# Smaller score tiles, sums in four column tiles, and a reordered weight part in a three-block layer stack

## The chip, the cores and the metric

One core of one Trainium2 chip. The metric is the device time of one execution in microseconds; the number given for a kernel is the median of its runs.

## What is computed

Three layers on 256 tokens of width 1024, in f32: an even block (HGRN2 scan and retention, then a squared-ReLU MLP), an odd block (mLSTM, then an MLP), and a hybrid layer (gated delta rule and block attention). The change touches the HGRN2 scan of the even block, some sums over partitions, and the preparation of a triangular inverse in the delta rule:

```python
def hgrn2_scan(q, k, logf, v):            # even block, 4 heads of 128, chunks of 64
    ...
        bcum = jnp.cumsum(lfc, axis=2)
        diff = bcum[:, :, :, None, :] - bcum[:, :, None, :, :]
        decay = jnp.exp(jnp.where(mask[:, :, None], diff, -jnp.inf))
        scores = jnp.einsum('bhtd,bhsd,bhtsd->bhts', qc, kc, decay)
...
    f = lb + (1.0 - lb) * jax.nn.sigmoid(hf)      # q = silu(hq), k = 1 - f, logf = log(f)
...
    # gated delta rule (hybrid layer), chunks of 64
    a = jnp.where(strict, jnp.einsum('bhnid,bhnjd->bhnij', k_beta, kf) * decay, 0.0)
    t_inv = lax.linalg.triangular_solve(eye + a, eye, left_side=True, lower=True)
```

## The kernel before, in words

**Projections.** The program is one fixed order per engine, written out by hand. All weights are cut into tiles of 128 partitions by 2048 columns (1 MB), loaded by SP into five slots `raw`. Every tile is split in two: ScalarE writes the high part `w_hi` (`split_until` of the scalar block, L1408, four slots), VectorE subtracts it from the tile and writes the low part `w_lo` (`split_until` of the vector block, L1915, 2.3 us each). TensorE multiplies by the high part first (`high_tile`) and, after a wait for the low part (`low_tile`), by that. Feature-major projections (`project_feature_major`, L583, L584 and the low part L591) serve hf, hq, rq, rk and, in the last block, dk, dq, dv, bq, bk; token-major ones (`project_token_major`, L625, L626, low part L632) serve the rest. Each projection has two weight tiles, named here bk.0 and bk.1. Where in VectorE's order the low part of a tile stands is said by a call `split_until(n)`, which makes all low parts up to tile n.

**Scores of the even block.** The 64x64 decayed score blocks can't be one product, since the decay depends on the feature. They are summed over levels m = 1, 2, 4, ... 128: for a pair of neighbouring runs of m tokens, the query side is scaled by exp(b - b at the edge) and the key side by exp(b at the edge - b). For each level VectorE writes the exponents into `D` (`diffs`, L2152 and L2153, one instruction for each half of the pairs), ScalarE takes exp (`level_exp`, L1617), VectorE multiplies by q and k into `Z0` or `Z1` (`scaled`, L2179 and L2180), TensorE makes the scores (`level_scores`, L965 for levels 0 to 6, blocks of 64x64: 16 matmuls of 128 rows by 64 columns, in two column tiles), and VectorE takes from them what the level's mask selects (`keep`, L2201, a predicated copy of 512 columns). Level 0 is q and k undecayed. The levels stand between the halves of the projections hi to rv0, from 38 to 100 us. Before them come the forget gate f (four instructions L2132, from it k by L2136), its logarithm (ScalarE, L1609), the scans of b (L2141) and the scaling of q (L2208).

**Sums over partitions** are matmuls with a column of ones as the moving side: four conditioning sums (`ada_sum`, L884, 8 matmuls each, between the products of the first and second MLP), the denominators of the odd block (L1108, 24 matmuls) and two sums of squares (`sum_squares` of the tensor block, L1140, 16 each). All use 64 stationary columns.

**The inverse in the delta rule.** VectorE multiplies keys' products by decays (`at`, L2567), copies the 32x32 diagonal blocks into the compact tile `ac` (L2569, four copies of 32 partitions), announces `at_ready`, makes the first inverse `Y32` (L2573, L2575) and its transpose `X` (L2576). GpSimd masks the compact tile for four levels (L546, `am_ready`). Before this it adds three shifted copies for a convolution (L537) and clears two areas with memsets (L541, L542, `zero_ready`). TensorE meanwhile projects bq and bk, transposes v (`dvt`, L1156) and then, between the halves of bv and bz, makes the small products with `X`, masks and `Y32` (L1227, L1233: 32x32 matmuls in four tiles; L1241, L1249, L1254 on the larger levels). In VectorE's order the low part of bk.0 (`split_until(LAST["dv"] + 3)`) stands behind the transpose.

Of the kernel before, what the change touches and what calls it, by code (L numbers as in the profile page):

```python
# [30 lines left out]
H = 4  # L31
# [192 lines left out]
E_AT = dict(qs=0, k=1024, b=2048, D=3072, Z0=4096, Z1=5120, scd=6144, sco=7168, vhg=7680, rq=8704, rk=9728,  # L224
# [19 lines left out]
def build(nc, weights, cols, rows, const, const_even, masks, x_in, out, stop=None):  # L244
    with ExitStack() as ctx:
# [190 lines left out]
        f_gate_ready = sem("f_gate_ready")  # L436
# [89 lines left out]
        def _(pool):  # L526
# [3 lines left out]
            for i in range({"even": 1, "mlp0": 2, "odd": 3, "mlp1": 4}.get(stop, 6)):  # L530
                if i == 5:
# [22 lines left out]
        def _(pe):  # L554
# [321 lines left out]
            def ada_sum(name):  # L876
# [63 lines left out]
            def level_scores(l):  # L940
# [162 lines left out]
            for t in range(TT):  # L1103
                for h in range(H):
                    for s in range(t + 1):
                        for b in range(2):
                            o = pair("mden")[64 * b:64 * b + 64, t * H + h:t * H + h + 1]
                            mm = pe.matmul(o, pt(h, s, t)[:, 64 * b:64 * b + 64], ones[:, 0:1], start=(s == 0), stop=(s == t))  # L1108
# [26 lines left out]
            def sum_squares(src):  # L1135

                after(l2_sq)
                for i in range(8):
                    for b in range(2):
                        mm = pe.matmul(acc[64 * b:64 * b + 64, i:i + 1], at(src, 64, i * P + 64 * b), ones[:, 0:1],  # L1140
# [60 lines left out]
            head_transposes("dvt", "v")  # L1201
            after(at_ready)
            fill("bk", 1)
# [185 lines left out]
        def _(act):  # L1389
# [218 lines left out]
            after(f_gate_ready)  # L1608
            act.activation(ev("D"), ev("Z0"), ACT.Ln).then_inc(logf_ready, 1)  # L1609
# [5 lines left out]
            def level_exp():  # L1615
                after(diff_ready)
                act.activation(ev("D"), ev("D"), ACT.Exp).then_inc(decay_ready, 1)  # L1617
# [29 lines left out]
            level_exp()  # L1647
            split_until(9)
            scaled_out("hi", by_token(ev("vhg")))
            level_exp()  # L1650
            split_until(10)
            level_exp()
            split_until(11)
            level_exp()
            scaled_out("hg", by_token(ev("ghg")), ACT.Silu)
            split_until(12)
            level_exp()
            split_until(13)
            level_exp()
            split_until(14)  # L1660
            swap_halves("rq")
            level_exp()
            split_until(15)
            level_exp()
# [215 lines left out]
        def _(dve):  # L1880
# [230 lines left out]
            def forget_bound():  # L2111
# [5 lines left out]
                link(dve.tensor_scalar(stat[:, 60:64], stat[:, 84:88], -1.0, 1.0, ALU.mult, ALU.add))  # L2117
# [12 lines left out]
            after(z0_ready)  # L2130
            for h in range(H):
                ins = dve.tensor_scalar(ev("Z0", T, h * T), ev("Z0", T, h * T), stat[:, 60 + h:61 + h], stat[:, 84 + h:85 + h],  # L2132
                                        ALU.mult, ALU.add)
            ins.then_inc(f_gate_ready, 1)
            dve.wait_ge(f_gate_ready, 1)
# [608 lines left out]
```

## Time and profile before

| | |
|---|---|
| median of 3 runs | 891.84 us (891.81 to 892.28) |
| profiled execution | 891.87 us, of it 890.1 us from the first to the last instruction |
| mean granted TensorE clock | 0.996 |
| PE / DVE / ACT / POOL busy | 878.5 / 644.6 / 497.4 / 21.6 us |
| DMA | 165.48 MB, mean 186 GB/s |

PE is TensorE, DVE VectorE, ACT ScalarE, POOL GpSimd; L12 is line 12 of the kernel. Rows of a timeline begin with start and length in microseconds; an f32 matmul shows as two passes, so 16 matmuls are x32.

### The profile page before, as it was taken

To read this page: it belongs to the slowest core of one execution; us is meant where nothing else is said; L and a number is where in the kernel's file an instruction comes from. 1 tells how busy PE (TensorE), PEld (TensorE's weight loads), DVE (VectorE), ACT (ScalarE), POOL (GpSimd) and SP (SyncE) were. 2 spreads that over 40 slices of the span, in tenths; PEclk is the share of its full clock that TensorE was granted. 3 is DMA by queue.
4 is the path that set the end of the run, shared out by engine and by line. 5 is a ranking of instruction groups with operands and counts; after the bars stand their busy time and mean duration, and the time that the engine had idled before them with its cause. 6 is when DMAs were issued, how large, how long until landed. Compare 5 with 4: busy or idle time off the path is not lost.

```text
span 890.1 us, 13545 instructions
## 1 busy us (share of the span) xinstructions
PE 878.5 (99%) x5714; PEld 749.5 (84%) x5714; DVE 644.6 (72%) x793; ACT 497.4 (56%) x678; POOL 21.6 (2%) x21
## 2 busy tenths in 40 slices
PE   9999999999999999999999999999999989999997
PEld 7889888888888888898888888888879988788885
DVE  6999656569777776699576977776677894556655
ACT  6875557466444444666566644445468764466624
POOL 0000000000000000000000000000000070000000
PEclk9999999999999999999999999999999999999999
DMA  9745444466666665454346666666446424434331
GB/s 363 275 143 176 156 142 141 143 236 221 239 232 236 235 238 184 173 182 148 137 142 230 227 236 235 236 239 237 147 154 236 143 95 149 144 120 158 135 128 48
DMA packets 24172, 165.48 MB, mean 186 GB/s; under 512 B 2688, under 2 KB 2944, under 8 KB 4912
## 3 DMA queue, kind: packets, MB, share of 16 engines
q1 hardware_dynamic: 22608, 159.74, 50.2%
q0 software_dynamic: 1072, 4.39, 1.3%
q8 instruction: 45, 0.74, 0.3%
q10 hardware_dynamic: 432, 0.49, 0.2%
q14 instruction: 15, 0.12, 0.0%
HBM read 163.56 MB, written 1.05 MB: 185 GB/s over the span
## 4 chain that ended last, share of the span: by engine, by line
PE 88%; DVE 8%; ACT 2%; issue 1%; DVEq 0%; ACTq 0%
PE acc L643 30%; PE lin L604 11%; PE lin L625 6%; PE lin L609 6%; PE lin L632 6%; PE lin L626 6%; DVE w_lo L1915 3%; PE lin L591 3%; PE lin L583 3%; PE lin L584 3%; PE acc L851 1%; PE acc L735 1%; PE acc L736 1%; DVE arena L2368 1%; ACT w_hi L1408 1%; PE acc L745 1%
## 5 line engine op out<-in xcount | busy, mean ns | idle before, releaser
L1915 DVE TENSOR_TENSOR w_lo<-raw,w_hi 128x2048 fp32r<-128x2048 f32 x137 | 315.0, 2313 | 141.6 <-ACT w_hi L1408 140.9
L1408 ACT CAST w_hi<-raw 128x2048 fp32r<-128x2048 f32 x137 | 259.5, 1907 | 137.1 <-DMA raw<-in_weights 89.8
L643 PE MATMUL acc<-w_hi,f_hi 128*128 128x512 f32 x288 | 113.2, 393 | 0.0
L643 PE MATMUL acc<-w_hi,f_lo 128*128 128x512 f32 x288 | 112.4, 390 | 0.0
L625 PE MATMUL lin<-w_hi,h_both 128*128 128x512 f32 x272 | 110.0, 404 | 0.6 <-ACT arena L1630 0.5
L604 PE MATMUL lin<-h_both,w_hi 128*128 128x512 f32 x448 | 106.7, 390 | 0.0
L626 PE MATMUL lin<-w_hi,h_both 128*128 128x512 f32 x272 | 106.3, 391 | 0.0
L604 PEld LDWEIGHTS lin<-h_both,w_hi 128*128 128x128 f32 x448 | 83.2, 188 | 16.8
L643 PE MATMUL acc<-w_lo,f_hi 128*128 128x512 f32 x288 | 79.0, 389 | 0.0
L632 PE MATMUL lin<-w_lo,h_both 128*128 128x512 f32 x272 | 69.2, 390 | 0.2 <-DVE w_lo L1915 0.2
L583 PE MATMUL lin<-h_both,w_hi 128*128 128x256 f32 x272 | 67.3, 287 | 0.0
L584 PE MATMUL lin<-h_both,w_hi 128*128 128x256 f32 x272 | 66.1, 283 | 0.0
L643 PEld LDWEIGHTS acc<-w_lo,f_hi 128*128 128x128 f32 x288 | 54.1, 188 | 11.3
L643 PEld LDWEIGHTS acc<-w_hi,f_hi 128*128 128x128 f32 x288 | 54.1, 188 | 10.8 <-DVE f_lo L2326 0.2
L643 PEld LDWEIGHTS acc<-w_hi,f_lo 128*128 128x128 f32 x288 | 54.1, 188 | 10.7
L625 PEld LDWEIGHTS lin<-w_hi,h_both 128*128 128x128 f32 x272 | 51.1, 188 | 12.3 <-issue 0.7
L632 PEld LDWEIGHTS lin<-w_lo,h_both 128*128 128x128 f32 x272 | 50.9, 188 | 11.5 <-DVE w_lo L1915 0.9
L626 PEld LDWEIGHTS lin<-w_hi,h_both 128*128 128x128 f32 x272 | 51.1, 188 | 9.7
L609 PEld LDWEIGHTS lin<-h_both,w_lo 128*128 128x128 f32 x448 | 57.4, 191 | 2.2
L643 PE MATMUL acc<-w_hi,h_both 128*128 128x512 f32 x224 | 58.2, 393 | 0.0
L609 PE MATMUL lin<-h_both,w_lo 128*128 128x256 f32 x448 | 58.1, 283 | 0.0
L583 PEld LDWEIGHTS lin<-h_both,w_hi 128*128 128x128 f32 x272 | 52.1, 191 | 0.3
(382 smaller groups left out, 1197.0 us busy)
## 6 DMA issues: line engine op xcount, KB each, us to landing
raw<-in_weights SPq DMA_DIRECT2D x149, 1024.0 KB, 4.8
rowbuf<-in_rows POOLq DMA_DIRECT2D x6, 512.0 KB, 4.0
x<-in_x_in SPq DMA_DIRECT2D x2, 512.0 KB, 4.4
raw<-in_weights SPq DMA_DIRECT2D x2, 512.0 KB, 6.7
arena<-in_const_even POOLq DMA_DIRECT2D x1, 1024.0 KB, 11.8
out<-x SPq DMA_DIRECT2D x3, 256.0 KB, 2.1
cst<-in_const SPq DMA_DIRECT2D x1, 596.0 KB, 10.0
out<-x ACTq DMA_DIRECT2D x1, 256.0 KB, 2.1
```

Of the source, the lines that this page charges most:

```text
L583: pe.matmul(o, hi[:, w], h[0], start=b == 0 and k == 0, stop=False)
L584: pe.matmul(o, hi[:, w], h[1], start=False, stop=False)
L591: mm = pe.matmul(pair(name)[:, (2 * i + b) * T:(2 * i + b + 1) * T], lo[:, w], chunk(k)[0], start=False, stop=b == 1 and k == DC - 1)
L604: pe.matmul(pair(out)[:, b * 512:(b + 1) * 512], hi[:, k * 256 + b * P:k * 256 + (b + 1) * P], h_both[:, k, :, :].rearrange("p a t -> p (a ...
L609: mm = pe.matmul(pair(out)[:, b * 512:b * 512 + T], lo[:, k * 256 + b * P:k * 256 + (b + 1) * P], h_hi[:, k, :], start=False, stop=k == DC ...
L625: pe.matmul(o, h[0], hi[:, w], start=i == 0 and k == 0, stop=False)
L626: pe.matmul(o, h[1], hi[:, w], start=False, stop=False)
L632: mm = pe.matmul(pair(name)[:, t * 512:(t + 1) * 512], chunk(4 * i + k)[0][:, t * P:(t + 1) * P], lo[:, k * 512:(k + 1) * 512], start=Fals ...
L643: return pe.matmul(acc[:, at:at + 512], part_of(2 * j + k)[i][:, t * P:(t + 1) * P], w[:, k * 1024 + c * 512:k * 1024 + (c + 1) * 512], st ...
L735: pe.matmul(lead_sum(t), h_hi[:, k, t * P:(t + 1) * P], w, start=k == 0, stop=False)
L1408: act.copy(w_hi[:, o % SPLIT, :], raw[:, j % RAW, :]).then_inc(hi_done, 1)
L1915: dve.tensor_tensor(w_lo[:, j % RAW, :], r, hi.bitcast(F32), ALU.subtract).then_inc(tile_split, 1)
```

## The change

1. `level_scores`: levels 0 to 5 in blocks of 32x32, 32 matmuls of 128 rows by 32 columns in four column tiles; level 6 by its 32x32 off-diagonal blocks alone, 16 matmuls in two column tiles; levels 7 and 8 as before. `keep` works on 256 columns; the level 6 blocks are copied straight to their place, and the near blocks are put there at level 7 by four small copies.
2. `ada_sum`, the denominators and `sum_squares`: four column tiles of 32 instead of two of 64, so twice the matmuls.
3. `diffs` is one instruction over both halves; the signs go into the scale of two exponentials; `scaled` is one product over both halves, which reads q and k through one access pattern (their places are swapped for it). At levels 7 and 8 copies of b go: the exponential reads b itself.
4. f is no longer written: ScalarE takes Ln(scale * sigmoid + bias) per head, VectorE makes k from the sigmoid in four instructions.
5. Last block: bk.0's low part ahead of the compact copies on VectorE; GpSimd's memsets behind its mask products; TensorE's wait for the compact tile behind bk.1.

```diff
@@ pool
-                    pool.memset(arena[:, S_AT["Y"]:S_AT["Y"] + 1024], 0.0)
-                    pool.memset(arena[0:64, S_AT["X64"]:S_AT["X64"] + 512], 0.0).then_inc(zero_ready, 1)
                     pool.wait_ge(at_ready, 1)
                     for l in range(2, 6):
...
+                    pool.memset(arena[:, S_AT["Y"]:S_AT["Y"] + 1024], 0.0)
+                    pool.memset(arena[0:64, S_AT["X64"]:S_AT["X64"] + 512], 0.0).then_inc(zero_ready, 1)
@@ ada_sum (the denominators and sum_squares in the same way)
-                    for b in range(2):
-                        at = c * P + 64 * b
-                        mm = pe.matmul(pair(name)[64 * b:64 * b + 64, c:c + 1], a[:, at:at + 64], ones[:, 0:1], start=True, stop=True)
+                    for r in range(4):
+                        at = c * P + 32 * r
+                        mm = pe.matmul(pair(name)[32 * r:32 * r + 32, c:c + 1], a[:, at:at + 32], ones[:, 0:1], start=True, stop=True)
@@ level_scores
+                elif l == 6:
+                    for i in range(8):
+                        for b in range(2):
+                            o = acc[64 * b:64 * b + 32, a + 32 * i:a + 32 * (i + 1)]
+                            c = i * P + 64 * b
+                            mm = pe.matmul(o, k[:, c:c + 32], q[:, c + 32:c + 64], start=True, stop=True)
                 else:
                     for i in range(8):
-                        for b in range(2):
-                            o = acc[64 * b:64 * b + 64, a + 64 * i:a + 64 * (i + 1)]
-                            c = i * P + 64 * b
-                            mm = pe.matmul(o, k[:, c:c + 64], q[:, c:c + 64], start=True, stop=True)
+                        for r in range(4):
+                            o = acc[32 * r:32 * r + 32, a + 32 * i:a + 32 * (i + 1)]
+                            c = i * P + 32 * r
+                            mm = pe.matmul(o, k[:, c:c + 32], q[:, c:c + 32], start=True, stop=True)
@@ tensor, last block
             head_transposes("dvt", "v")
+            fill("bk", 1)
             after(at_ready)
-            fill("bk", 1)
@@ scalar
-            act.activation(ev("D"), ev("Z0"), ACT.Ln).then_inc(logf_ready, 1)
+            for h in range(H):
+                ins = act.activation(ev("D", T, h * T), ev("Z0", T, h * T), ACT.Ln, scale=stat[:, 60 + h:61 + h],
+                                     bias=stat[:, 84 + h:85 + h])
...
+                if m < 64:
+                    d = ev("D").rearrange("p (n a m) -> p n a m", a=2, m=m)
+                    act.activation(d[:, :, 1, :], d[:, :, 1, :], ACT.Exp)
+                    act.activation(d[:, :, 0, :], d[:, :, 0, :], ACT.Exp, scale=-1.0).then_inc(decay_ready, 1)
+                    return
@@ vector, diffs and scaled
-                    edge = b[:, :, 0, m - 1:m].to_broadcast([P, n, m])
-                    dve.tensor_tensor(d[:, :, 1, :], b[:, :, 1, :], edge, ALU.subtract)
-                    dve.tensor_tensor(d[:, :, 0, :], edge, b[:, :, 0, :], ALU.subtract).then_inc(diff_ready, 1)
+                    edge = b[:, :, m - 1:m].to_broadcast([P, n, 2 * m])
+                    dve.tensor_tensor(d, b, edge, ALU.subtract).then_inc(diff_ready, 1)
...
-                dve.tensor_tensor(z[:, :, 1, :], d[:, :, 1, :], q[:, :, 1, :], ALU.mult)
-                dve.tensor_tensor(z[:, :, 0, :], d[:, :, 0, :], k[:, :, 0, :], ALU.mult).then_inc(z_ready, 1)
+                kq = ev("k", 2 * (1024 + m)).rearrange("p (a r) -> p a r", a=2)[:, :, 0:1024]
+                kq = kq.rearrange("p a (n x m) -> p n a x m", x=2, m=m)[:, :, :, 0, :]
+                dve.tensor_tensor(z, d, kq, ALU.mult).then_inc(z_ready, 1)
@@ vector, keep
-                dve.copy_predicated(ev("sco", 512).rearrange("p (n t) -> p n t", n=8), msk_l, src).then_inc(level_free, 1)
+                msk_l = small_mask(l).to_broadcast([P, 8, 32])
+                dve.copy_predicated(near.rearrange("p (n t) -> p n t", n=8), msk_l, src).then_inc(level_free, 1)
@@ vector, last block
             link(dve.tensor_tensor(at("at"), at("at"), acc[:, 0:1024], ALU.mult))
+            split_until(LAST["dv"] + 3)
             for r in range(4):
                 ins = dve.tensor_copy(compact(at("ac", 256), r), small_blocks(at("at"), r))
...
-            split_until(LAST["dv"] + 3)
             split_until(LAST["bq"] + 3)
```

What moves, on the engines it concerns. VectorE in the last block, from the second product of the scores to q's scaling, before (`w_lo<-raw,w_hi` is a weight tile's low part, here bk.0, bk.1, bv.0):

```order
L2566 TENSOR_TENSOR arena<-arena,acc 128x1024 [waits sc_done]
L2567 TENSOR_TENSOR arena<-arena,acc 128x1024
L2569 COPY arena<-arena 32x256 [waits dve_step]
L2569 COPY arena<-arena 32x256 x3
L2573 TENSOR_TENSOR arena<-arena,msk 128x256 [waits at_ready]
L2575 TENSOR_TENSOR arena<-cst,arena 128x256 [waits dve_step]
L2576 STREAM_TRANSPOSE arena<-arena 128x256 [waits dve_step]
L1915 TENSOR_TENSOR w_lo<-raw,w_hi 128x2048 [waits hi_done] x3
L2583 TENSOR_TENSOR arena<-arena 128x512 [waits deg_read,l2_done]
```

and the same piece in the changed kernel:

```order
L2594 TENSOR_TENSOR arena<-arena,acc 128x1024 [waits sc_done]
L2595 TENSOR_TENSOR arena<-arena,acc 128x1024
L1941 TENSOR_TENSOR w_lo<-raw,w_hi 128x2048 [waits hi_done,dve_step]
L2598 COPY arena<-arena 32x256 x4
L2602 TENSOR_TENSOR arena<-arena,msk 128x256 [waits at_ready]
L2604 TENSOR_TENSOR arena<-cst,arena 128x256 [waits dve_step]
L2605 STREAM_TRANSPOSE arena<-arena 128x256 [waits dve_step]
L1941 TENSOR_TENSOR w_lo<-raw,w_hi 128x2048 [waits hi_done] x2
L2611 TENSOR_TENSOR arena<-arena 128x512 [waits deg_read,l2_done]
```

One low part of three has moved ahead of the four copies, and everything from the copies to the transpose stands behind it. GpSimd in the same place, before:

```order
L537 TENSOR_TENSOR arena<-arena 128x4x253 [waits taps_ready,v_conv]
L541 MEMSET arena 128x1024 [waits even_loaded,v_conv]
L542 MEMSET arena 64x512
L546 TENSOR_TENSOR arena<-arena,msk 128x256 [waits at_ready]
L546 TENSOR_TENSOR arena<-arena,msk 128x256 x3
```

and changed:

```order
L537 TENSOR_TENSOR arena<-arena 128x4x253 [waits taps_ready,v_conv]
L544 TENSOR_TENSOR arena<-arena,msk 128x256 [waits at_ready,even_loaded,v_conv]
L544 TENSOR_TENSOR arena<-arena,msk 128x256 x3
L545 MEMSET arena 128x1024
L546 MEMSET arena 64x512
```

The memsets now follow the four mask products. VectorE in the even block, from the scans of b to the exponents of level 2, before:

```order
L2141 SCALAR_TENSOR_TENSOR arena<-cst,arena 128x256 x4
L2152 TENSOR_TENSOR arena<-arena 128x512
L2153 TENSOR_TENSOR arena<-arena 128x512
L2208 TENSOR_TENSOR arena<-lin,arena 128x1024
L1915 TENSOR_TENSOR w_lo<-raw,w_hi 128x2048 x3
L2179 TENSOR_TENSOR arena<-arena 128x512
L2180 TENSOR_TENSOR arena<-arena 128x512
L2152 TENSOR_TENSOR arena<-arena 128x256x2
L2153 TENSOR_TENSOR arena<-arena 128x256x2
L2201 COPY_PREDICATED arena<-msk,acc 128x512
```

and changed:

```order
L2166 SCALAR_TENSOR_TENSOR arena<-cst,arena 128x256 x4
L2176 TENSOR_TENSOR arena<-arena 128x1024
L2236 TENSOR_TENSOR arena<-lin,arena 128x1024
L1941 TENSOR_TENSOR w_lo<-raw,w_hi 128x2048 x3
L2202 TENSOR_TENSOR arena<-arena 128x1024
L2176 TENSOR_TENSOR arena<-arena 128x1024
L2229 COPY_PREDICATED arena<-msk,acc 128x256
```

The order is the same; pairs of instructions have become one, and the predicated copy is half as wide.

## Rows read from the trace of the kernel before

**Rows 1.** The page, part 1: busy us (share of the span) xinstructions.
```profile
PE 878.5 (99%) x5714; PEld 749.5 (84%) x5714; DVE 644.6 (72%) x793; ACT 497.4 (56%) x678; POOL 21.6 (2%) x21
```

**Rows 2.** Waits of TensorE: us in total, times, longest us; first and fifth of eight.
```profile
PE lin L591 <- DVE w_lo L1915: 2.4, 1, 2.4
...
PE acc L1254 <- DVE arena L2599: 0.3, 1, 0.3
```

**Rows 3.** Timeline of TensorE, even block: start us, us, instruction, xcount.
```profile
36.37 2.14 PE L632 MATMUL lin<-w_lo,h_both 128*128 128x512 f32 x8
38.44 1.15 PE L965 MATMUL acc<-arena 128*64 128x64 f32 x32
...
51.94 1.15 PE L965 MATMUL acc<-arena 128*64 128x64 f32 x32
```

**Rows 4.** Timeline of TensorE, last block: 32x32 matmuls in four tiles, two, one.
```profile
747.99 0.75 PE L1227 MATMUL acc<-arena 32*32 32x32 f32 x64
...
769.75 0.69 PE L1241 MATMUL acc<-arena 32*32 32x32 f32 x32
...
773.85 0.57 PE L1249 MATMUL acc<-arena 32*32 32x32 f32 x13
```

**Rows 5.** Timeline of TensorE: sums over partitions.
```profile
253.65 0.63 PE L884 MATMUL lin<-cst,ada_acc 128*64 128x1 f32 x16
...
432.02 1.57 PE L1108 MATMUL lin<-cst,arena 128*64 128x1 f32 x48
...
682.56 1.10 PE L1140 MATMUL acc<-cst,arena 128*64 128x1 f32 x32
```

**Rows 6.** Timeline of VectorE, last block: low parts and the compact copies.
```profile
715.29 4.54 DVE L1915 TENSOR_TENSOR w_lo<-raw,w_hi 128x2048 fp32r<-128x2048 f32 x1
...
722.13 3.73 DVE L2569 COPY arena<-arena 32x256 f32<-32x256 f32 x4
...
727.54 2.28 DVE L1915 TENSOR_TENSOR w_lo<-raw,w_hi 128x2048 fp32r<-128x2048 f32 x1
```

**Rows 7.** The chain that ended last: low parts of bk.0 and bk.1.
```profile
729.88 3.59 PE lin L591 x16
738.29 1.93 PE lin L591 x16
```

**Rows 8.** Stretches: us, busy us (x) of PE, PEld, DVE, ACT, POOL, PEclk, DMA share, GB/s.
```profile
725.00:730.00 5.00, 2.61 (x22) 2.41 (x22) 4.88 (x7) 4.14 (x6) 4.47 (x4) 1.00 0.53 195
730.00:735.00 5.00, 5.00 (x30) 5.00 (x31) 5.00 (x2) 0.52 (x3) 3.03 (x2) 0.66 0.17 28
```

**Rows 9.** GpSimd: its additions by line (ns min/median/max, first and last start), then its timeline.
```profile
L537 POOL TENSOR_TENSOR arena<-arena x3: 1982/2397/3937, 715.3 to 721.8; 128x1020 f32<-128x1020 f32 x1, 128x1016 f32<-128x1016 f32 x1, 128x1012 f32<-128x1012 f32 x1
...
723.82 0.98 POOL L541 MEMSET arena<- 128x1024 f32 x1
724.74 0.67 POOL L542 MEMSET arena<- 64x512 f32 x1
725.94 7.09 POOL L546 TENSOR_TENSOR arena<-arena,msk 128x256 f32<-128x256 f32 x4 [0.53 <-DVE arena L2569]
```

**Rows 10.** Timeline of VectorE, even block.
```profile
34.03 6.69 DVE L1915 TENSOR_TENSOR w_lo<-raw,w_hi 128x2048 fp32r<-128x2048 f32 x3
...
48.15 0.69 DVE L2180 TENSOR_TENSOR arena<-arena 128x512 f32<-128x512 f32 x1
...
50.09 0.74 DVE L2201 COPY_PREDICATED arena<-msk,acc 128x512 f32<-128x512 uint16 x1
...
58.58 1.22 DVE L2232 TENSOR_TENSOR arena<-arena 128x1024 f32<-128x1024 f32 x1
```

**Rows 11.** Timeline of ScalarE: the logarithm, and four activations with a column scale.
```profile
27.60 1.06 ACT L1609 ACTIVATE arena<-arena 128x1024 f32<-128x1024 f32 x1
...
718.50 1.71 ACT L1797 ACTIVATE arena<-arena,colbuf 128x256 f32<-128x256 f32 x4
```

**Rows 12.** One stretch of the even block, columns as in rows 8.
```profile
30.00:60.00 30.00, 30.00 (x250) 24.51 (x250) 28.03 (x29) 22.91 (x20) 0.00 (x0) 1.00 0.49 169
```

More of the change, by code:

```diff
@@ L434, in build @@
         s_out = sem("s_out")
-        f_gate_ready = sem("f_gate_ready")
+        bound_ready = sem("bound_ready")
         logf_ready = sem("logf_ready")
@@ L1105, in _ @@
                     for s in range(t + 1):
-                        for b in range(2):
-                            o = pair("mden")[64 * b:64 * b + 64, t * H + h:t * H + h + 1]
-                            mm = pe.matmul(o, pt(h, s, t)[:, 64 * b:64 * b + 64], ones[:, 0:1], start=(s == 0), stop=(s == t))
+                        for r in range(4):
+                            o = pair("mden")[32 * r:32 * r + 32, t * H + h:t * H + h + 1]
+                            mm = pe.matmul(o, pt(h, s, t)[:, 32 * r:32 * r + 32], ones[:, 0:1], start=(s == 0), stop=(s == t))
             mm.then_inc(lin_special, 1)
@@ L1138, in sum_squares @@
                 for i in range(8):
-                    for b in range(2):
-                        mm = pe.matmul(acc[64 * b:64 * b + 64, i:i + 1], at(src, 64, i * P + 64 * b), ones[:, 0:1],
+                    for r in range(4):
+                        mm = pe.matmul(acc[32 * r:32 * r + 32, i:i + 1], at(src, 32, i * P + 32 * r), ones[:, 0:1],
                                        start=True, stop=True)
@@ L1613, in _, with level_exp @@
             ahead("hq")
-            def level_exp():
+            def level_exp(l):
                 after(diff_ready)
-                act.activation(ev("D"), ev("D"), ACT.Exp).then_inc(decay_ready, 1)
+                m = (LEVELS + [128])[l - 1]
+                if m < 64:
[3 more added lines that the diff above has]
+                    return
+                b, d = (ev(x).rearrange("p (h c m) -> p h c m", c=4, m=64) for x in ("b", "D"))
+                if m == 64:
+                    for c in (0, 2):
+                        act.activation(d[:, :, c + 1, :], b[:, :, c + 1, :], ACT.Exp)
+                    d = ev("D").rearrange("p (n a m) -> p n a m", a=2, m=m)
+                    act.activation(d[:, :, 0, :], d[:, :, 0, :], ACT.Exp).then_inc(decay_ready, 1)
+                else:
+                    act.activation(d[:, :, 2, :], b[:, :, 2, :], ACT.Exp)
+                    act.activation(d[:, :, 0:2, :], d[:, :, 0:2, :], ACT.Exp)
+                    act.activation(d[:, :, 3, :], d[:, :, 3, :], ACT.Exp).then_inc(decay_ready, 1)
             def swap_halves(name):
@@ L2161, in diffs @@
                     for c in (0, 2):
-                        dve.tensor_tensor(d[:, :, c, :], end(c), b[:, :, c, :], ALU.subtract)
-                        ins = dve.tensor_copy(d[:, :, c + 1, :], b[:, :, c + 1, :])
+                        ins = dve.tensor_tensor(d[:, :, c, :], end(c), b[:, :, c, :], ALU.subtract)
                 else:
@@ L2177, in scaled @@
                     dve.wait_ge(level_done, l - 1)
[L2178 to L2180 removed]
+                z, d = (ev(x).rearrange("p (n a m) -> p n a m", a=2, m=m) for x in (f"Z{l % 2}", "D"))
+                kq = ev("k", 2 * (1024 + m)).rearrange("p (a r) -> p a r", a=2)[:, :, 0:1024]
+                kq = kq.rearrange("p a (n x m) -> p n a x m", x=2, m=m)[:, :, :, 0, :]
+                dve.tensor_tensor(z, d, kq, ALU.mult).then_inc(z_ready, 1)
                 dve.wait_ge(z_ready, l + 1)
[L2183 to L2184 removed]
+            near = ev("sco", 256)
             def keep(l):
@@ L2193, in keep @@
                 if l == 7:
-                    for b in range(2):
-                        link(dve.tensor_copy(own_blocks(ev("scd"), b), low_levels(b)))
+                    for r in range(4):
+                        ins = dve.tensor_copy(small_blocks(ev("scd"), r), compact(near, r))
+                    link(ins)
                     upper = acc[0:64, a:a + 512].rearrange("p (n t) -> p n t", n=8)
@@ L2198, in keep @@
                     return
-                src = acc[:, a:a + 512].rearrange("p (n t) -> p n t", n=8)
-                msk_l = level_mask(l).rearrange("p (o t) -> p o t", o=1).to_broadcast([P, 8, 64])
-                dve.copy_predicated(ev("sco", 512).rearrange("p (n t) -> p n t", n=8), msk_l, src).then_inc(level_free, 1)
+                src = acc[:, a:a + 256].rearrange("p (n t) -> p n t", n=8)
+                if l == 6:
+                    for b in range(2):
+                        dst = ev("scd")[64 * b:64 * b + 32, :].rearrange("p (n t) -> p n t", n=8)[:, :, 64 * b + 32:64 * b + 64]
+                        ins = dve.tensor_copy(dst, src[64 * b:64 * b + 32, :, :])
+                    ins.then_inc(level_free, 1)
+                    return
+                msk_l = small_mask(l).to_broadcast([P, 8, 32])
+                dve.copy_predicated(near.rearrange("p (n t) -> p n t", n=8), msk_l, src).then_inc(level_free, 1)
                 dve.wait_ge(level_free, l + 1)
```

40 lines of the change are left out of this document (18 added, 22 removed).

## The prediction, made before the changed kernel ran

> **What bounds the kernel now.** I read the page's shares first: TensorE has matmuls in flight in 99% of the span, VectorE works 72% of it, ScalarE 56% [rows 1]. Then the waits of TensorE: the list has eight lines, 5.6 us together, and its first, 2.4 us for a low weight part, is nearly half of that [rows 2]. So what TensorE issues sets the time. A microsecond off TensorE's own work is a microsecond off the end, wherever VectorE and ScalarE can follow; a microsecond off the other two is worth nothing, except in front of that one wait. The sum is made against the profiled execution, 891.87 us (890.1 of span and 1.8 around it); the median of the runs shown, 891.84, is the same for this purpose. A difference under 0.2% (1.8 us) can't be told from none here.
>
> **Small matmuls.** Every f32 matmul appears as two passes. A 64-wide score level is 16 matmuls, 32 passes, and its row spans 1.15 us with a last pass of 0.22: a pass starts every (1.15 - 0.22)/31 = 0.030 us [rows 3]. These are two column tiles that run side by side on the same 128 rows. How fast 32-wide tiles go is seen in the last block, where tiles of 32 rows by 32 columns are used: four tiles in turn make (0.75 - 0.19)/63 = 0.0089 us per pass, two make (0.69 - 0.19)/31 = 0.0161, one makes (0.57 - 0.19)/12 = 0.032 [rows 4]. So one tile takes 0.032 us for its pass and the tiles overlap. The new shape, 128 rows by 32 columns, stands in no row. Its upper neighbour is the pair of 64-wide tiles (0.030 per pass), its lower one the four 32x32 tiles (0.0089). I take 0.0089 for four column tiles, because the 64-wide pair already shows that column tiles on shared rows overlap; both ends stay for the range.
> - Levels 0 to 5: 16 matmuls become 32, 64 passes; the row becomes 63 x 0.0089 + 0.19 = 0.75 us. 6 x (1.15 - 0.75) = **2.40 us** saved.
> - Level 6: 16 matmuls stay, now 32 wide in two column tiles. By the two-tile row 0.69 us: **0.46 us** saved. Levels 7 and 8 are unchanged.
> - Sums over partitions have one moving column, and the rows show that this doesn't help: they too start a pass every 0.029 us [rows 5], so the 64-wide stationary side sets the pace, not the moving one. In four tiles: four conditioning sums, 15 x 0.029 = 0.44 becomes 31 x 0.0089 = 0.28, **0.64** in all; the denominators, 47 x 0.029 = 1.37 becomes 95 x 0.0089 = 0.85, **0.52**; two sums of squares, 31 x 0.029 = 0.90 becomes 0.56, **0.68**.
> Together 4.70 us of TensorE.
>
> The Trainium skill speaks against this part: "TensorEngine Tiling (Array Packing)", Performance Considerations, warns not to take a tiling factor from a dimension that is small already, since every matmul carries some 60 cycles, and "TensorE: Matmul & The Clock Gate", Part 1, says that starts never come closer than about 25 ns. The trace of this kernel disagrees for 32x32 tiles (8.9 ns between starts). By that rule the six levels and the sums, 736 passes, would take an estimated 18.4 us of starts and the forecast would end near 895.
>
> **The low part ahead of the compact copies.** VectorE works in order. Between the products L2567 and the low part of bk.0 stand four copies into the compact tile (3.73 us), two small operations and a transpose; the low part starts at 727.54 and ends at 729.82 [rows 6]. TensorE had finished the high half of bk.0 at 727.5 and waits 2.4 us for it, until 729.88 [rows 2, 7]. The clock follows: the granted clock is 1.00 in 725 to 730 and 0.66 in 730 to 735, a mean over the two levels of 2.4 and 1.2 GHz [rows 8], and the 16 matmuls behind the wait take 3.59 us, where the 16 of bk.1 take 1.93 [rows 7]: 1.66 too much.
>
> After the change this subtraction is at the head, at 722.13. GpSimd's third shifted addition starts at 721.8 and takes 1.98 us [rows 9], and beside such additions VectorE's subtraction of bq.1 took 4.54 us for what otherwise takes 2.28 [rows 6]; the first copy suffers from the same now. So I let the moved subtraction wait until 723.8 and end at 726.05. TensorE comes for it at 727.5, less what it gains by then over VectorE, at most the 0.34 us of the second sum of squares. The margin is about 1 us: the wait goes, **2.4 + 1.66 = 4.06 us**. Late next are the copies. The two memsets of GpSimd (0.98 and 0.67 us) that ran beside them are now behind its four mask products, so the copies take at most the old 3.73: the compact tile is ready between 726.1 and 729.8 instead of 725.9, X 1.7 us later (725.86 to 727.54 now), the first mask about a quarter of 7.09 later [rows 6, 9]. TensorE comes for bk.1's low part at 727.5 + 1.93 + 4.82 = 734.2 (the last term is what lies between the low parts of bk.0 and bk.1 now, 738.29 - 729.88 - 3.59 [rows 7]), and for the first small products two us behind that. The low part of bk.1, behind the transpose, ends between 730 and 734: enough, but this is the margin to look at. The cleared areas are wanted only from 769 on, and GpSimd is through at about 738. TensorE's wait for the compact tile moves behind bk.1 and costs nothing for the same reason.
>
> **The even block's VectorE and ScalarE work.** Differences of both halves in one: 0.69 + 0.69 (1.30 by the starts) becomes about 1.22, the row of one 1024-wide product; the products z the same; the predicated copy of 512 columns, 0.74, halves to some 0.4; copies at levels 7 and 8 go, the four small ones at level 7 replace two of 0.42. That is some 3 us less for VectorE between 30 and 100 us, where it is nearly full (28.03 us of 30 in the first stretch) [rows 12]. All of it is costed at nothing for the end: VectorE had z for level 2 ready at 48.8 and TensorE wanted it at 51.9 [rows 3, 10]; if that cover were gone, each 0.1 us would count once per level. ScalarE's logarithm in four pieces with a column as scale and bias costs 1.71 instead of 1.06, by the row of four 256-wide activations with a column scale [rows 11], so 0.22 for each added instruction; its exponential in two or three pieces is then 0.2 to 0.4 us longer per level, hidden by the same 3 us. The logarithm has no such cover: scans, differences and q behind it end about 0.1 us later, and TensorE takes the low part of hi.0 at 36.37, when VectorE has just finished it (34.03 plus a third of 6.69 = 36.26) [rows 3, 10]. I give 0.1 us for this and 0.1 for the other short waits [rows 2] that become longer when TensorE comes earlier.
>
> Sum: 4.70 + 4.06 - 0.2 = 8.56 us. 891.87 - 8.56 = **883.3 us**.
>
> **The rivals.**
> A. *Four column tiles on shared rows don't run four wide.* Each tile needs all 128 partitions read for itself. If what limits the 64-wide pair is columns delivered per microsecond (64 in 0.029), a 32-wide pass costs 0.0145, levels 0 to 5 and all sums gain nothing, and only level 6 and the wait do: 891.87 - 4.06 - 0.46 + 0.2 = 887.6. For it: passes with 1 and with 64 moving columns cost the same. Against: the clean overlap of the 32x32 tiles [rows 4], though these lie on different rows.
> B. *A wait comes back.* The moved subtraction, held up by GpSimd, or bk.1's low part comes late enough to idle TensorE and lower its clock again: the 4.06 us are lost, 891.87 - 4.70 + 0.2 = 887.4. Against: the margins of 1 and of 0 to 4 us above. With A as well it is 891.6, no change.
> C. *A floor between starts for tiles of 128 rows, whatever their width.* The 0.029 with one moving column could be that floor. Then twice the passes cost twice the time: levels 0 to 5, 6 x (63 x 0.029 + 0.19 - 1.15) = 5.2; conditioning sums 4 x 0.46 = 1.9; denominators 1.4; sums of squares 2 x 0.93 = 1.9: 10.4 us more, 4.06 less, 898.2, slower than before. It decides from a pass of about 0.020 us on: there 736 passes and their tails eat the 4.06 and level 6's 0.46. Against: one 32x32 tile alone needs 0.032 and four need 0.0089 each, which no floor allows, unless it belongs to tiles of 128 rows.
> The Trainium skill's 25 ns is a milder form of C and shares its chance.
>
> **How the numbers follow.** Forecast 0.70, since two independent pieces of it rest on rows; A 0.12; B 0.10; A and B together 0.03; C 0.05. Faster by over 0.2%: forecast, A and B, 0.92. Same: 0.03. Slower: 0.05. The range reaches from 882.3 (a pass every 0.032/4 = 0.008 us, 0.7 less, and no new short waits) to 887.9, which takes in A and B.
>
> **What would show it.** Score rows of levels 0 to 5 at x64 with 0.75 us each, level 6 at 0.69, denominators x96 near 1.0; at 1.1 us a level it is A, at 2.0 it is C. No wait of TensorE for the low part of bk.0, granted clock 1.00 throughout from 10 to 880 us, and L591 of bk.0 at 1.9 us. On VectorE, bk.0's subtraction ends before TensorE's high half does, and the copies follow it. Wrong would be: a new line in TensorE's waits over 0.5 us, in the even block (ScalarE's pieces) or at bk.1, or a saved 4.7 us that turns up as idle time ahead of a low part.

## The result, and the profile after

The changed kernel takes 883.54 us (median of 5 runs, 883.44 to 884.02), the kernel before 891.84: a ratio of 0.9912 with a 95% interval of 0.9900 to 0.9923. In a later round, beside the experiments, it took 883.43 (883.31 to 883.56). The profiled execution took 883.74 us, 881.9 of it span. Beside the experiments the kernel before took 891.5 to 893.1 us in 28 executions, with a mean granted clock of at most 0.997, and 890.2 to 890.4 us in 11, with 0.998 or 0.999 (one more, at 1082.8 us and 0.752, is left out), so the 8.3 us are a difference from the more frequent group.

The page, part 1, of the changed kernel (answers to [rows 1]):

```profile
PE 871.8 (99%) x6082; PEld 742.3 (84%) x6082; DVE 640.2 (73%) x779; ACT 499.6 (57%) x691; POOL 21.3 (2%) x21
```

TensorE is busy for 6.7 us less, with 368 passes more. Its waits, five of nine lines (to [rows 2]): the 2.4 us for bk.0's low part are gone, and L632 has grown from 0.2 to 0.4. The two lines of L895 are waits for the first loads; another trace of the same kernel, that of experiment 6, has neither.

```profile
PE lin L625 <- ACT arena L1656: 0.5, 1, 0.5
PE lin L632 <- DVE w_lo L1941: 0.4, 2, 0.2
PE acc L895 <- DMA x<-in_x_in: 0.4, 1, 0.4
PE acc L1260 <- DVE arena L2627: 0.3, 1, 0.3
...
PE acc L895 <- DMA cst<-in_const: 0.2, 1, 0.2
```

Its timeline: hi.0's low part, a score level (L971), level 6 (L965), a conditioning sum, the denominators, a sum of squares (to [rows 3, 5]).

```profile
36.85 1.45 PE L632 MATMUL lin<-w_lo,h_both 128*128 128x512 f32 x5 [0.24 <-DVE w_lo L1941]
38.92 0.76 PE L971 MATMUL acc<-arena 128*32 128x32 f32 x64
...
83.72 0.70 PE L965 MATMUL acc<-arena 128*32 128x32 f32 x32
...
251.40 0.43 PE L884 MATMUL lin<-cst,ada_acc 128*32 128x1 f32 x32
...
429.19 0.98 PE L1114 MATMUL lin<-cst,arena 128*32 128x1 f32 x96
...
678.88 0.71 PE L1146 MATMUL acc<-cst,arena 128*32 128x1 f32 x64
```

The level's row is (0.76 - 0.20)/63 = 0.0089 us per pass, the denominators' (0.98 - 0.17)/95 = 0.0085, a last pass of 0.20 or 0.17 taken off. Four column tiles on the same 128 rows start passes as closely as the four 32x32 tiles did before. The first line is new: 0.24 us of wait for hi.0's low part.

The chain that ended last and the stretches, around bk.0 (to [rows 7, 8]): its 16 low matmuls take 1.92 us, and the clock stays at its upper level.

```profile
723.39 1.92 PE lin L591 x16
...
730.02 1.93 PE lin L591 x16
```

```profile
715.00:725.00 10.00, 10.00 (x85) 10.00 (x85) 9.82 (x12) 8.04 (x11) 6.50 (x5) 1.00 0.56 207
725.00:730.00 5.00, 5.00 (x45) 5.00 (x44) 5.00 (x3) 3.85 (x10) 5.00 (x3) 1.00 0.65 211
```

VectorE's timeline there, then GpSimd's (to [rows 6, 9]):

```profile
717.78 3.75 DVE L1941 TENSOR_TENSOR w_lo<-raw,w_hi 128x2048 fp32r<-128x2048 f32 x1
721.46 1.18 DVE L2598 COPY arena<-arena 32x256 f32<-32x256 f32 x4
...
723.95 0.45 DVE L2605 STREAM_TRANSPOSE arena<-arena 128x256 f32<-128x256 f32 x1
724.32 4.96 DVE L1941 TENSOR_TENSOR w_lo<-raw,w_hi 128x2048 fp32r<-128x2048 f32 x2
```

```profile
722.81 7.00 POOL L544 TENSOR_TENSOR arena<-arena,msk 128x256 f32<-128x256 f32 x4 [3.42 <-DVE arena L2598]
729.76 0.96 POOL L545 MEMSET arena<- 128x1024 f32 x1
730.65 0.52 POOL L546 MEMSET arena<- 64x512 f32 x1
```

The moved subtraction takes 3.75 us, stretched by GpSimd's addition, and ends at 721.5; TensorE comes for it at 723.2. The four copies, with nothing of GpSimd beside them, take 1.18 us instead of 3.73.

The even block, where the new 0.24 us come from: ScalarE's logarithm, then VectorE's scans, differences and q (to [rows 11, 10]).

```profile
27.65 2.08 ACT L1617 ACTIVATE arena<-arena,stat 128x256 f32<-128x256 f32 x4
```

```profile
29.77 2.44 DVE L2166 TENSOR_TENSOR_SCAN arena<-cst,arena 128x256 f32<-128x256 f32 x4 [1.03 <-ACT arena L1617]
32.24 1.23 DVE L2176 TENSOR_TENSOR arena<-arena 128x1024 f32<-128x1024 f32 x1
33.38 1.22 DVE L2236 TENSOR_TENSOR arena<-lin,arena 128x1024 f32<-128x1024 f32 x1
34.51 6.69 DVE L1941 TENSOR_TENSOR w_lo<-raw,w_hi 128x2048 fp32r<-128x2048 f32 x3
```

Four logarithms with columns as scale and bias take 2.08 us, not the 1.71 of activations with a scale column alone. VectorE now waits for them, and q is scaled half a microsecond later than before (33.38 us for 32.89), the low part behind it as well.

### The profile page after: what moved, and what is told of

It is laid out like the page before. It is cut to its first block, busy times and chain, and to the rows that moved or that the text cites. A ratio compares the mean times of both kernels' runs of the same rounds, so it can differ in the third digit from the quotient of the medians.

```text
span 881.9 us, 14281 instructions
## 1 busy us (share of the span) xinstructions
PE 871.8 (99%) x6082; PEld 742.3 (84%) x6082; DVE 640.2 (73%) x779; ACT 499.6 (57%) x691; POOL 21.3 (2%) x21
## 3 DMA queue, kind: packets, MB, share of 16 engines
HBM read 163.56 MB, written 1.05 MB: 187 GB/s over the span
## 4 chain that ended last, share of the span: by engine, by line
PE 88%; DVE 7%; ACT 3%; issue 1%; DMA 1%; DVEq 0%; SPq 0%; ACTq 0%
PE acc L643 30%; PE lin L604 12%; PE lin L625 6%; PE lin L609 6%; PE lin L632 6%; PE lin L626 6%; PE lin L583 3%; DVE w_lo L1941 3%; PE lin L584 3%; PE lin L591 3%; PE acc L851 1%; PE acc L735 1%; PE acc L736 1%; DVE arena L2396 1%; ACT w_hi L1414 1%
## 5 line engine op out<-in xcount | busy, mean ns | idle before, releaser
L632 PE MATMUL lin<-w_lo,h_both 128*128 128x512 f32 x272 | 69.2, 390 | 0.4 <-DVE w_lo L1941 0.4
L632 PEld LDWEIGHTS lin<-w_lo,h_both 128*128 128x128 f32 x272 | 50.9, 188 | 11.9 <-DVE w_lo L1941 1.3
```

Source lines behind the costliest of these rows:

```text
L632: mm = pe.matmul(pair(name)[:, t * 512:(t + 1) * 512], chunk(4 * i + k)[0][:, t * P:(t + 1) * P], lo[:, k * 512:(k + 1) * 512], start=Fals ...
```

## Experiments

Theory: the gain is TensorE's own shorter rows plus the vanished wait with its slow clock, and all else is covered. Rivals: one of the two is worth nothing and the other more, or VectorE's relief did it. Medians of 4 to 5 runs (11 for the exchanged loops); the changed kernel, 883.43 and 883.54 in two rounds, is the mark, and the runs of one version spread by 0.1 to 0.7 us. The experiments ran on four chips, and the mark beside them on one of these alone (experiment 6 and the first trials of 7); the medians of the kernel before on the four, 891.78 to 891.93, agree within 0.15 us, so versions on different chips are compared to a few tenths at best. Ratios are to the kernel before. Every kernel does the whole computation.

**1. The low part back** in its old place, in the changed kernel.

```diff
-            split_until(LAST["dv"] + 3)
             for r in range(4):
                 ins = dve.tensor_copy(compact(at("ac", 256), r), small_blocks(at("at"), r))
...
             dve.transpose(at("X", 256), at("Y32", 256)).then_inc(X_ready, 1)
+            split_until(LAST["dv"] + 3)
             split_until(LAST["bq"] + 3)
```

> The changed kernel with bk.0's low part back behind the transpose, all else as changed. Theory: in the changed kernel TensorE comes for this low part at 723.2 us. With the copies first again, held up by GpSimd's addition until 719.4, but with no memset beside them, the low part would end at about 724.6, so TensorE waits about 1.4 us: 883.5 + 1.4 = 884.9 us if the granted clock stays at 1.00, up to 1.7 more (886.6) if it falls behind the wait as it did before. Rival (the order on VectorE was worth nothing, the gain was in the matmuls): 883.5.

Measured 885.09 us (884.86 to 885.35), ratio to before 0.993 (0.9918 to 0.9942): 1.6 more than the changed kernel, near the 1.4 of the theory without a fall of the clock. Timelines of VectorE and TensorE, and the stretch:

```profile
718.20 2.67 DVE L2597 COPY arena<-arena 32x256 f32<-32x256 f32 x4
```

```profile
724.88 2.18 PE L591 MATMUL lin<-h_both,w_lo 128*128 128x256 f32 x16 [1.05 <-DVE w_lo L1941]
```

```profile
725.00:730.00 5.00, 5.00 (x43) 5.00 (x44) 5.00 (x2) 2.52 (x10) 4.39 (x4) 1.00 0.34 113
```

The copies are 1.1 us shorter than before without the memsets beside them (2.67 for 3.73), so the wait is 1.05 us instead of 2.4, and after 1.05 us of idle the granted clock did not fall. The row behind the wait is 2.18 us long, where the same row in the changed kernel takes 1.92: this wait cost some 0.25 us more than its idle time, at the upper clock. So the rows give 1.3 us for the move and the runs 1.6. This profiled execution was also 0.4 us late before it came to the place (its first matmul of hi.0 starts at 33.22 us, that of the changed kernel at 32.80); in the trace of experiment 6, the changed kernel again, it is 32.55, so this start isn't the same in every execution. That moving the memsets alone would have brought the rest is read off these rows; it was not run.

**2. The low part moved alone**, in the kernel before (the same edit the other way).

> The kernel before with this one move alone: bk.0's low part ahead of the compact copies on VectorE, memsets and matmuls untouched. Theory: the wait of 2.4 us and the half clock behind it (1.7 us) go: 891.8 - 4.1 = 887.7 us, and the granted clock is 1.00 from 10 to 880 us. Rival 1 (the wait only moves on to bk.1's low part or to the compact tile): 889 to 892 with a new wait of TensorE there. Rival 2 (the clock fall has another cause than the wait): 889.4, with a stretch of half clock that stays.

Measured 887.65 us (887.53 to 888.14), ratio 0.9959 (0.9947 to 0.9972): 4.1 less than before, to a tenth what was expected. TensorE's waits have no L591 any more, and the stretch that had 0.66 has 1.00:

```profile
730.00:735.00 5.00, 5.00 (x45) 5.00 (x43) 5.00 (x4) 3.97 (x9) 4.13 (x2) 1.00 0.62 211
```

No wait took its place in the last block, and the half clock went with the wait. The two can now be priced apart. Between the start of bk.0's low row and the end of the transposes of v behind it lie 4.57 us in the kernel before (3.59 and 0.98) and 3.05 in experiment 1 (2.18 and 0.87), which had a wait but no half clock: the clock costs 1.5 us, the wait 2.4 and 0.25. The 11 executions of the kernel before with the higher mean clock are 1.6 us shorter (medians of 890.3 and 891.9), about what the fall costs; it was probably missing there. No trace of one was kept, so this is not shown.

**3. The sums in two column tiles again**, in the changed kernel; one of three places:

```diff
-                    for r in range(4):
-                        at = c * P + 32 * r
-                        mm = pe.matmul(pair(name)[32 * r:32 * r + 32, c:c + 1], a[:, at:at + 32], ones[:, 0:1], start=True, stop=True)
+                    for b in range(2):
+                        at = c * P + 64 * b
+                        mm = pe.matmul(pair(name)[64 * b:64 * b + 64, c:c + 1], a[:, at:at + 64], ones[:, 0:1], start=True, stop=True)
```

> The changed kernel with all sums over partitions in two column tiles of 64 again. By the starts of the passes in the two traces (29.1 ns before, 8.5 now): conditioning sums 4 x 0.20, denominators 0.59, sums of squares 2 x 0.39 = 2.2 us more: 885.7 us. Rival (sums that stand ahead of a wait give nothing back): the two sums of squares and the denominators cost nothing, only the conditioning sums do: 884.3.

Measured 885.36 us (885.26 to 885.85), ratio 0.9935 (0.9921 to 0.9948): 1.8 to 1.9 more, where starts alone gave 2.2 and the rival 0.8. Counted to the start of the next matmul, the rows of its trace are 2.16 us longer (0.56 for 0.36 four times, 1.49 for 0.91, 1.03 for 0.64 twice). The sums give back most of their time; where the other 0.3 us went is not shown.

**4. Score levels in 64x64 blocks again**, in the changed kernel, with the predicated copies that belong to them (`level_scores` for levels 0 to 6 and `keep` as before).

> The changed kernel with the scores of levels 0 to 6 in 64x64 blocks and the predicated copies of 512 columns as before; sums, logarithm, merged instructions and the moved low part as changed. Theory: per level 0 to 5 the last pass starts 0.93 us behind the first instead of 0.57, and the next matmul 0.152 behind it instead of 0.126, so 0.39 each; level 6 0.93 instead of 0.50, 0.45: 2.8 us more, 883.5 + 2.8 = 886.3. Rival (VectorE, loaded with 0.3 us more per predicated copy, now makes TensorE wait): over 887, with waits in the even block.

Measured 886.38 us (886.34 to 886.66), ratio 0.9945 (0.9932 to 0.9958): 2.8 to 2.9 more, as expected. The wait for hi.0 is there too (0.24 us), and no other has come in the even block, so it doesn't hang on the tiles.

**5. Column tile after column tile.** The same 32 matmuls a level, the loops exchanged.

```diff
-                    for i in range(8):
-                        for r in range(4):
+                    for r in range(4):
+                        for i in range(8):
```

> The changed kernel with the loops of levels 0 to 5 exchanged: all eight 32x32 blocks of one column tile, then the next, so neighbours in the order use the same tile. Same 32 matmuls. Theory: the tiles overlap only when neighbouring instructions go to different tiles; a pass every 0.032 us as in the row of one 32x32 tile, 63 x 0.032 + 0.2 = 2.2 us a level instead of 0.77: 6 x 1.4 = 8.6 us more: 892.1. Rival (TensorE picks matmuls of other tiles ahead out of its queue): a level stays near 0.77, total 883.5.

Measured 890.36 us (890.18 to 890.92), ratio 0.999 (0.9982 to 0.9999): 6.8 to 6.9 more, most of what the change had won and far above the 2.8 that the smaller blocks gave: in this order they are slower than the old 64x64 blocks (1.91 us a level for 1.15). TensorE's timeline, a level:

```profile
39.08 1.91 PE L971 MATMUL acc<-arena 128*32 128x32 f32 x64
```

That is (1.91 - 0.20)/63 = 0.027 us per pass instead of 0.0089, and six levels times 1.15 us make the 6.9. The overlap comes from neighbours in the order going to different tiles, and the engine did not look ahead for them. The expectation had 0.032 from a 32-row tile; a tile of 128 rows is faster, 0.027. Four tiles in turn are thus three times as quick as one, not four times; what holds them at 0.0089 is not shown.

**6. The mark again, and halves apart.** The even block's differences, exponentials and products as before the change.

```diff
-                    b, d = (ev(x).rearrange("p (n c) -> p n c", n=n) for x in ("b", "D"))
-                    edge = b[:, :, m - 1:m].to_broadcast([P, n, 2 * m])
-                    dve.tensor_tensor(d, b, edge, ALU.subtract).then_inc(diff_ready, 1)
+                    b = ev("b").rearrange("p (n a m) -> p n a m", a=2, m=m)
+                    d = ev("D").rearrange("p (n a m) -> p n a m", a=2, m=m)
+                    edge = b[:, :, 0, m - 1:m].to_broadcast([P, n, m])
+                    dve.tensor_tensor(d[:, :, 1, :], b[:, :, 1, :], edge, ALU.subtract)
+                    dve.tensor_tensor(d[:, :, 0, :], edge, b[:, :, 0, :], ALU.subtract).then_inc(diff_ready, 1)
...
```

> The changed kernel itself, as the mark for the runs beside it on the same chip: 883.5 us.

Measured 883.43 us (883.31 to 883.56), ratio 0.9907 (0.9893 to 0.9920).

> The changed kernel with the even block's differences, exponentials and products as before (two differences and two products of half the size a level, one exponential over all, the copies at levels 7 and 8 back); score tiles, predicated copies and logarithm as changed. Theory: the merged instructions were worth nothing for the end, since z is ready about 3 us before TensorE wants it: 883.5, within 0.3. Rival (VectorE is nearly full between 30 and 90 us, so its 3 us less are what let TensorE come earlier): up to 1 to 2 us slower, with waits of TensorE for VectorE in the even block.

Measured 883.61 us (883.43 to 883.88), ratio 0.9909 (0.9895 to 0.9922): 0.2 more than the mark beside it, and the two sets of runs overlap. Point 3 of the change is worth nothing that is clear of the spread. Its instructions did get cheaper: VectorE's timeline with the halves apart, then that of the changed kernel, for the same level.

```profile
60.58 0.69 DVE L2161 TENSOR_TENSOR arena<-arena 128x512 f32<-128x512 f32 x1
61.19 0.68 DVE L2162 TENSOR_TENSOR arena<-arena 128x512 f32<-128x512 f32 x1
```

```profile
60.50 1.23 DVE L2176 TENSOR_TENSOR arena<-arena 128x1024 f32<-128x1024 f32 x1
61.64 0.44 DVE L2229 COPY_PREDICATED arena<-msk,acc 128x256 f32<-128x256 uint16 x1
```

The narrower predicated copies stay here, and the merged instructions stay in experiment 4; no run takes both away. It is shown that VectorE can do without either of them, and not that it can do without both.

**7. Can the new 0.24 us go?** First trial: q's scaling ahead of level 1's differences.

```diff
-            diffs(1)
             filled(dve, "hq")
             dve.tensor_tensor(by_head(ev("qs")), by_head(pair("hq")[:, :]), every, ALU.mult).then_inc(freed("hq"), 1)
+            diffs(1)
```

> The changed kernel with the differences of level 1 behind the scaling of q. In the changed kernel TensorE waits 0.24 us for hi.0's low part, because the logarithm in four pieces (2.08 us) delays scans, differences and q. Theory: q's scaling starts at 32.9 instead of 33.4, and the wait shrinks to at most 0.1 us: 883.3. Rival: the scans still end too late, or the exponentials of level 1 come late instead: 883.5.

Measured 884.35 us (884.32 to 884.38), ratio 0.9917 (0.9903 to 0.9930): 0.9 slower than the mark, against the expectation. VectorE's timeline and TensorE's:

```profile
32.85 1.22 DVE L2235 TENSOR_TENSOR arena<-lin,arena 128x1024 f32<-128x1024 f32 x1 [0.90 <-PE lin L591]
33.99 1.22 DVE L2176 TENSOR_TENSOR arena<-arena 128x1024 f32<-128x1024 f32 x1
35.12 6.69 DVE L1941 TENSOR_TENSOR w_lo<-raw,w_hi 128x2048 fp32r<-128x2048 f32 x3
```

```profile
37.46 2.14 PE L632 MATMUL lin<-w_lo,h_both 128*128 128x512 f32 x8 [1.10 <-DVE w_lo L1941]
```

VectorE now idles 0.90 us for TensorE's hq and does the differences between q and the low part that TensorE wants. The expectation looked at q, which is not what TensorE waits for. The wait grew from 0.24 to 1.10, which is the 0.9.

Level 7 in pairs of tiles, on top of this:

```diff
-                        o = acc[0:64, a + 64 * i:a + 64 * (i + 1)]
+                        p0, c0 = 64 * (i % 2), 64 * (i // 2)
+                        o = acc[p0:p0 + 64, a + c0:a + c0 + 64]
...
```

> The one before with level 7's eight matmuls of 64 columns alternating between both column tiles (odd blocks to the upper 64 partitions, two copies out instead of one). Theory: passes at 0.029 us as in other pairs of 64-wide tiles instead of 0.0615: 15 x 0.032 = 0.48 us less than without it: 882.8. Rival (the longer copy out delays the next level or the heads' outputs): no gain, 883.3.

Measured 883.98 us (883.79 to 884.22), ratio 0.9913 (0.9899 to 0.9926): 0.4 less than the trial that it stands on (0.48 was expected). TensorE's timeline has level 7 in the changed kernel, in one tile, and then here, in two:

```profile
90.02 1.15 PE L959 MATMUL acc<-arena 128*64 128x64 f32 x16
```

```profile
90.71 0.69 PE L960 MATMUL acc<-arena 128*64 128x64 f32 x16
```

With a last pass of 0.22 taken off, that is 0.062 us per pass for one 64-wide tile and 0.031 for two.

Second trial: q, then the low part, then the differences, with level 7 in pairs kept.

```diff
             dve.tensor_tensor(by_head(ev("qs")), by_head(pair("hq")[:, :]), every, ALU.mult).then_inc(freed("hq"), 1)
+            split_until(LAST["hq"] + 1)
             diffs(1)
```

> The changed kernel with q's scaling, then hi.0's low part, then the differences of level 1 on VectorE, and level 7 in pairs of column tiles. In the trial with only q ahead, the differences stood between q and the low part, and TensorE waited 1.1 us. Theory: the low part now ends at 36.3, TensorE waits under 0.1 instead of 0.24 us; with 0.4 from level 7: 883.4 - 0.2 - 0.4 = 882.8. Rival: the exponential of level 1 comes late for level 1's scores and gives it back: 883.1 or more.

Measured 882.73 us (882.67 to 882.75), ratio 0.9903 (0.9889 to 0.9917): 0.7 less than the mark, as expected. TensorE has no idle time from 36 to 100 us in its trace, where the changed kernel has 0.24. VectorE's timeline:

```profile
34.08 2.28 DVE L1942 TENSOR_TENSOR w_lo<-raw,w_hi 128x2048 fp32r<-128x2048 f32 x1
36.28 1.22 DVE L2177 TENSOR_TENSOR arena<-arena 128x1024 f32<-128x1024 f32 x1
```

**8. The 0.49 us behind the first small products.**

```diff
             fill("bk", 0)
+            fill("bk", 1)
             after(silu_ready, 3)
             head_transposes("dvt", "v")
-            fill("bk", 1)
...
```

> c2 with the eight transposes of v behind both halves of bk on TensorE, and their scaled copies on ScalarE behind the first small product's copy. TensorE waits 0.49 us after the first small products, because bv opens the accumulator that ScalarE is still copying bk out of. Theory: with the transposes in between this copy is over in time: 882.8 - 0.5 = 882.3. Rival: ScalarE's eight scaled copies (2.2 us) in the new place delay a high part or the next copy, and a new wait shows up: 882.8 or more.

Measured 883.34 us (883.16 to 883.71), ratio 0.9912 (0.9898 to 0.9926): 0.6 slower than without it. The wait of 0.49 is gone, and another has come; ScalarE's timeline, then TensorE's:

```profile
732.01 2.18 ACT L1855 ACTIVATE arena<-lin,stat 128x128 f32<-128x128 f32 x8
734.02 1.96 ACT L1415 CAST w_hi<-raw 128x2048 fp32r<-128x2048 f32 x1
```

```profile
739.27 0.74 PE L1234 MATMUL acc<-arena 32*32 32x32 f32 x64 [1.01 <-DVE arena L2631]
```

The scaled copies delay bz.0's high part, this VectorE's low part, and that the transpose of the small inverse, which stands behind it in VectorE's order. Last trial, the copies behind the high part:

> The last trial with ScalarE's eight scaled copies of v behind bz.0's high part instead of ahead of it. In the last trial the wait of 0.49 us was gone, but these copies put bz.0's high part at 734.0 to 736.0, VectorE made its low part behind that and only then the next transpose, and TensorE waited 1.01 us for it. Theory: with the high part first (about 732 to 734) VectorE is through by 737.1 and TensorE wants the transpose at 738.3: no wait, 882.7 - 0.5 = 882.2. Rival: the scaled copies in this place delay the next copy out of the small products: 882.7 or more.

Measured 882.49 us (882.33 to 882.66), ratio 0.9897 (0.9881 to 0.9914). Neither wait is left, and it is the fastest version of all, 1.0 us under the changed kernel. Over the second trial, run on another chip, it gained 0.24 us, half of what was expected. Its profile shows both waits gone, but the first matmul of hi.0 starts 0.19 us later (32.83 for 32.64), behind the first loads. The two traces of the changed kernel itself differ by 0.25 there (32.80 and 32.55), so this much comes and goes with the execution. Between the two profiled executions, 882.73 and 882.39 us, the gain from there on is 0.34 + 0.19 = 0.53, the expected half microsecond.

## Why the prediction was right, and where it was off

The forecast was 883.3 us and 8.56 less; it is 883.54 and 8.3 less (891.84 - 883.54).

- *Small matmuls, 4.70 us.* By the runs, levels 2.8 to 2.9 (forecast 2.86) and sums 1.8 to 1.9 (1.84). For the sums this agreement is in part luck: their rows became 2.16 us shorter, more than forecast, and the runs show less than the rows. The choice that carried most of it, 0.0089 us a pass for a shape without a row, is confirmed by the row of the first level, 0.76 us; rival A would have shown 1.1 us there and C 2.0. The reason given, that 64-wide column tiles on shared rows already overlap, had no row, but holds: 0.062 us a pass in one, 0.030 in a pair. What the forecast leaves unsaid is the condition that experiment 5 shows, neighbours in the order in different tiles; and since one tile alone needs 0.027, the overlap is threefold, so the 0.008 at the lower end of the range was not reached by the levels. The Trainium skill's floor of about 25 ns between starts ("TensorE: Matmul & The Clock Gate", Part 1), cited against the change, does not hold for f32 in four column tiles: 8.9 and 8.5 ns. What it describes is near the 27 ns seen when neighbours share a tile. That the width of the stationary side sets the pace of the sums was right as well: with one moving column they went from 29.1 to 8.5 ns.
- *The low part, 4.06 us.* As a single edit of the kernel before it is worth 4.1. The forecast puts the whole 1.66 us of the longer row down to the clock; by experiments 1 and 2 the half clock costs 1.5 (1.4 in that row, the rest behind it) and 0.25 came with the wait of experiment 1 at the upper clock too. Where the clock probably didn't fall, the kernel before takes 890.3 us, and against that the whole change gains 6.8 us, not 8.3. The margin of about 1 us was too careful: the subtraction ended at 721.5 with TensorE at 723.2, 1.7 us. It took 3.75 us where the forecast allowed 3.92, and VectorE came forward at least as much as TensorE (the product ahead of it starts at 716.54 us, before at 720.89), where the forecast let TensorE gain 0.34 on it. The copies and bk.1's low part, the "margin to look at", never came near: 1.18 us of copies, and bk.1's low part at 726.6 with TensorE at 729.9. What the forecast did not see is that the memsets' move and the low part's move serve the same wait: with the memsets moved, the low part's place is worth 1.3 to 1.6.
- *Costed at nothing.* Right for the merged differences, exponentials and products (0.2 us, inside the spread). The cover is there still: z for level 2 is ready at 49.0 us, and TensorE wants it at 51.7.
- *"I give 0.1 us for this".* Off in size: the logarithm took 2.08 us, not 1.71, because the 0.22 per added instruction came from activations with a column as scale only; the wait was 0.24. By the starts the low part of hi.0 comes 4.05 us behind hi.0's first matmul, 3.68 before, so the term that was 0.1 is 0.37. That covers the 0.25 us between 883.3 and 883.54, but so would the start of the execution alone, which differs by as much between two traces of the same kernel. Three parts as measured by runs (2.8, 1.8 and 4.1) and the wait as read from the trace (-0.2) add up to 8.5, against 8.3 and 8.5 for the whole in two rounds. The logarithm was not run by itself, nor were the memsets.
- Rival B has nothing in the trace, rival C is ruled out.

## What to carry to other kernels

In this kernel small f32 matmuls are paid by the pass, and a pass by the width of its column tile (0.027 us for 32 columns, 0.062 for 64, one tile alone): cut them to 32 columns and send neighbours in the order to different column tiles, even where the moving side is a single column. In a kernel that TensorE bounds, look for the one place where it waits and ask what stands ahead of the producer on its engine; judge a reordering by what is waited for, not by the operation that looks late. Two edits in front of the same wait are not worth their sum.

## What was not expected of the hardware

- A wait of 2.4 us was followed by half the granted clock (0.66 over the next 5 us, 1.5 us lost). Waits of 1.05, 1.10 and 1.01 us in the experiments were not followed by it, with the clock at 1.00 in the stretch behind the first of them.
- VectorE and GpSimd took turns on work in SBUF: in the kernel before the subtraction of 2.28 us took 4.54, and GpSimd's second addition, started in the meantime, 3.94 for the 1.98 of the third; in the changed kernel the moved one took 3.75. Copies of 1.18 us took 2.67 behind one addition and 3.73 with the memsets as well. A product that takes one operand from `acc` was not slowed: 1.21 us at 719.76, beside the second addition.
- A tile of 128 rows and 32 columns starts a pass every 27 ns by itself, one of 32 rows and 32 columns every 32.
- Four activations of 256 columns took 1.34 us without such columns (the silu of v at 726.03 us in the kernel before), 1.71 with a column as scale, and 2.08 with columns for scale and bias.
